# Experts of a two-layer block: two of four token blocks gather their experts' rows, the other two go through all experts

## The chip, the cores and the metric

The kernel runs on one core of a Trainium2 chip. The metric is the time of one execution on the device in microseconds; all data is float32. In the text PE is TensorE (the matrix engine), DVE is VectorE, ACT is ScalarE, POOL is GpSimd, and SP is the queue engine that only issues transfers. Engines run their own instruction lists in order and wait for each other by semaphores.

## The reference, cut to what matters

The whole program is three mixing layers on 512 tokens of width 1024 (convolution, sparse attention, attention and a gated recurrence), then an expert layer, then a small gated layer (called ple). Only the expert layer is changed. There are 16384 experts, each with a row `u` and a row `v` of 1024 numbers. A token picks 16 experts in each of 8 heads, from the sums of two lists of 128 key scores:

```
q = (ht @ w_q).reshape(T, PEER_HEADS, 2, PEER_DKEY // 2)
s = jnp.einsum('thpc,hpnc->thpn', q, sub_keys, preferred_element_type=jnp.float32)
v1, i1 = lax.top_k(s[:, :, 0], K)
v2, i2 = lax.top_k(s[:, :, 1], K)
...
top_s, pos = lax.top_k(cand, K)
idx = jnp.take_along_axis(cand_idx, pos, axis=-1)
g = jax.nn.softmax(top_s, axis=-1)
...
ue = jnp.take(u, ib, axis=0)
a = jnp.einsum('thkd,td->thk', ue, xb, preferred_element_type=jnp.float32)
w = jax.nn.gelu(a) * gb
ve = jnp.take(v, ib, axis=0)
return jnp.einsum('thk,thkd->td', w.astype(ve.dtype), ve)
```

## The kernel before, in words

The 512 tokens are four blocks (b = 0 to 3) of 128 tokens, one token per partition. Everything up to the expert layer is bound to TensorE and stays as it is, apart from its last steps. At the end of the mixing layers PE makes, block by block, the last output product (`merge(b)`: transposes `mT`, then `out_c`), DVE adds it to the residual X (`residual_sum(b)`), normalises the block (`expert_rows(b)`), and PE multiplies by the query weights (`queries`: 32 products of 256 columns for two blocks, then 8 small products with the sub-keys, which give the scores of two heads).

Then comes the expert layer. DVE routes: a group is one head of one block, 32 groups in all, and `route_step(n, k)` does a sixteenth of a group's work (MAX8, FIND_INDEX8, MATCH_REPLACE8 and small operations on HOT). POOL gathers: one indirect transfer brings for the 128 tokens of a block the row `u` of one pick (128 rows of 4 KB, 512 KB), another the row `v`. There are 32 x 16 = 512 picks (PICKS), so 1024 gathers, into rings of 8 buffers each (`U_RING`, `V_RING`). For each pick DVE forms the 128 dot products with the normalised block (L2246), ACT and DVE turn them into weights (`activated`, `weigh`, `weighted`), ACT writes the 16 weights of a group one by one as diagonal matrices (L1446), and PE adds diagonal times gathered rows into PSUM (`expert_row`, L1017, two products of 512 columns per pick). The last of every three picks near the end are added by DVE (L2179). The ple layer follows for each block when its sums are complete (L1079, L1091, `ple_steps`); block 3 comes last, so its ple steps stand at the very end.

The order is written out by hand: DVE's list is one loop over the 512 picks, with the routing of the group two ahead between the dots; POOL's list issues `gather_u(u)` with the `gather_v` that fall due, each after a wait for the buffer.

## Time and profile before

| | us |
|---|---|
| median of 3 runs | 3231.74 (3227.18 to 3245.19) |
| the profiled execution, from its first to its last instruction | 3278.9 |
| PE, DVE, ACT, POOL busy in it | 2812.3, 1829.2, 652.2, 1273.9 |
| granted TensorE clock, mean | 0.967 of full speed |
| moved by transfers | 665.89 MB, 536.94 MB of it by the gathers |

The profiled execution is 47 us longer than the median of the timed runs. Busy time is what an engine spent in instructions; the time of a transfer is not that of the instruction that issues it.

### The profile page before, as it was taken

Reading aid. Unit: us, or ns where it says so; the run is one execution under the profiler, and the core shown is the slowest. Engines: PE = TensorE matmul, PEld = TensorE weight load, DVE = VectorE, ACT = ScalarE, POOL = GpSimd, SP = SyncE. Lnnn points to the kernel's source line nnn. Section 1 sums busy time; section 2 is a strip of 40 time slices with the busy share of each in tenths; the row PEclk is TensorE's granted clock in tenths of the full one; section 3 lists DMA queues with packets and bytes.
Section 4 is the critical chain, followed back from the end, with each engine's and each line's share of the span. In section 5 each row is a group of like instructions: output and inputs, shape, how many; then the busy total and the mean of one; then the engine's idle time right before and its main releaser. Section 6 shows DMA issues by size and latency. Waiting matters only on the chain.

```text
span 3278.9 us, 26326 instructions
## 1 busy us (share of the span) xinstructions
PE 2812.3 (86%) x7932; PEld 1338.4 (41%) x7932; DVE 1829.2 (56%) x4230; ACT 652.2 (20%) x1556; POOL 1273.9 (39%) x1113
## 2 busy tenths in 40 slices
PE   9999999998889899988898889777768786777778
PEld 4455445454554444555555334322223232222323
DVE  4989502058751322267529666576666666666643
ACT  1114301022320112344401111111111111111111
POOL 0520000000000000022104767777777777777774
...
GB/s 179 77 103 52 64 77 77 77 77 26 51 40 77 67 69 51 26 30 49 90 65 216 366 371 368 371 387 373 345 361 371 363 353 367 372 366 352 368 386 244
DMA packets 161469, 665.89 MB, mean 203 GB/s; under 512 B 17856, under 2 KB 18240, under 8 KB 154304
## 3 DMA queue, kind: packets, MB, share of 16 engines
q0 software_dynamic: 147456, 536.94, 43.9%
...
q14 instruction: 64, 0.52, 0.0%
...
## 4 chain that ended last, share of the span: by engine, by line
PE 54%; POOL 18%; issue 9%; DVE 9%; DMA 7%; ACT 2%; another core or an unknown queue 0%; DVEq 0%; ACTq 0%; POOLq 0%; SPq 0%
PE ps L537 13%; PE ps L1017 8%; POOL G L1567 8%; PE ps L652 6%; POOL H L1583 5%; POOL XT L1583 4%; PE ps L589 4%; PE ps L882 3%; DMA XT<-peer_v,C 3%; DMA H<-peer_v,C 3%; PE ps L790 2%; PE ps L911 2%; PE ps L819 2%; DMA G<-peer_u,C 2%; PE ps L976 2%
## 5 line engine op out<-in xcount | busy, mean ns | idle before, releaser
L2246 DVE CUSTOM_DVE_ANT_0 G<-G,H 128x1024 f32<-128x1024 f32 x512 | 627.7, 1226 | 465.7 <-DMA G<-peer_u,C 396.0
L1017 PE MATMUL ps<-H,MK 128*128 128x512 f32 x1196 | 591.2, 623 | 190.3 <-DMA H<-peer_v,C 124.0
L1567 POOL DMA_INDIRECT G<-peer_u,C x512 | 540.3, 1055 | 302.9 <-issue 151.8
L537 PE MATMUL ps<-XT,W 128*128 128x512 f32 (+1 forms) x1344 | 543.0, 553 | 8.9 <-issue 6.5
L1017 PE MATMUL ps<-XT,MK 128*128 128x512 f32 x812 | 403.1, 629 | 130.6 <-DMA XT<-peer_v,C 80.3
L1017 PEld LDWEIGHTS ps<-H,MK 128*128 128x128 f32 x1196 | 218.6, 195 | 532.3 <-issue 476.0
L1583 POOL DMA_INDIRECT H<-peer_v,C x304 | 350.6, 1153 | 131.3 <-issue 71.8
L537 PEld LDWEIGHTS ps<-XT,W 128*128 128x128 f32 x1344 | 254.1, 190 | 294.2 <-issue 286.2
L1017 PEld LDWEIGHTS ps<-XT,MK 128*128 128x128 f32 x812 | 149.5, 197 | 381.1 <-issue 326.0
L1542 POOL COPY PR<-H 128x256 f32<-128x256 f32 x4 | 1.4, 392 | 781.2 <-DVE H L1871 781.2
L1446 ACT ACTIVATE MK<-C 128x128 f32<-128x128 f32 x502 | 175.0, 393 | 524.5 <-PE ps L1017 292.6
L1583 POOL DMA_INDIRECT XT<-peer_v,C x208 | 241.1, 1159 | 78.7 <-issue 48.5
L652 PE MATMUL ps<-W,Y 128*128 128x512 f32 x512 | 226.1, 603 | 13.1 <-DVE Y L1746 6.1
L589 PE MATMUL ps<-XT,W 128*128 128x512 f32 x448 | 220.5, 604 | 1.6 <-ACT G L1152 1.6
L1554 POOL TENSOR_TENSOR H<-H 128x256 f32<-128x256 f32 x56 | 47.6, 852 | 353.9 <-ACT H L1376 320.6
L1645 DVE SCALAR_TENSOR_TENSOR Y<-H,V,Y x240 | 165.3, 765 | 0.0
L652 PEld LDWEIGHTS ps<-W,Y 128*128 128x128 f32 x512 | 98.3, 193 | 140.3 <-issue 137.1
L1433 ACT ACTIVATE H<-C 128x16 f32<-128x16 f32 x32 | 6.9, 216 | 630.3 <-DVE H L2162 336.8
L1528 POOL TENSOR_TENSOR H<-H,SIG 128x512 f32 x12 | 73.5, 6125 | 111.9 <-ACT SIG L1212 108.9
L1755 DVE SCALAR_TENSOR_TENSOR X<-X,H 128x512 f32<-128x512 f32 x16 | 11.1, 691 | 181.9 <-ACT H L1137 181.9
L589 PEld LDWEIGHTS ps<-XT,W 128*128 128x128 f32 x448 | 80.6, 195 | 59.7 <-issue 55.7
L882 PE MATMUL ps<-W,XT 128*128 128x512 f32 x192 | 98.5, 622 | 0.3 <-issue 0.3
...
## 6 DMA issues: line engine op xcount, KB each, us to landing
...
G<-peer_u,C POOLq DMA_INDIRECT x512
...
```

What stands on the lines that cost most here:

```text
L537: mm = pe.matmul(b[:, 0:rhs[k].shape[-1]], w[:, k, m * P:(m + 1) * P], rhs[k], start=(k == 0), stop=(k == KD - 1))
L589: mm = pe.matmul(FILL_BANK[j % 2][:, :], w[:, k, m * P:(m + 1) * P], XT[:, k, :], start=(k == 0), stop=(k == KD - 1))
L652: mm = pe.matmul(ps[pos % 4][:, :], Y[:, (j * KD + k) * T + b * P:(j * KD + k) * T + (b + 1) * P], w[:, k, :], start=(j == 0 and k == 0), ...
L790: mm = pe.matmul(ps[p0 % 4][:, 0:n], XT[:, k, b * P:(b + 1) * P], w[:, k, 0:n], start=(k == 0), stop=(k == KD - 1))
L882: mm = pe.matmul(ring(pos)[:, :], XT[:, k, b * P:(b + 1) * P], w[:, k, :], start=(k == 0), stop=(k == KD - 1))
L1017: mm = pe.matmul(ps[2 * b + half][:, :], DG[by_tensor(v - 1) % DIAG_RING], VB[at][:, half * T:(half + 1) * T], start=(n == FIRST[b] and k ...
L1446: act.activation(DG[at % DIAG_RING], ident, ACT.Copy, scale=GW[:, v:v + 1]).then_inc(diag_full, 1)
L1528: pool.tensor_tensor(hrow(i * 4 + j, TAPS - 1, T), hrow(i * 4 + j, TAPS - 1, T), SIG[:, j, :], ALU.mult).then_inc(glu_done, 1)
L1567: pool.indirect_dma_start(UB[u % U_RING], None, peer_u, bass.IndirectOffsetOnAxis(ap=IDX[:, u:u + 1], axis=0)).then_inc(u_loaded[u % U_RIN ...
L1583: pool.indirect_dma_start(VB[at], None, peer_v, bass.IndirectOffsetOnAxis(ap=IDX[:, v:v + 1], axis=0)).then_inc(v_loaded[at], 16)
L1645: ins = dve.scalar_tensor_tensor(yt(c), hrow(c, k, T), V[:, ds(c * TAPS + (FM["conv_w"] + k), 1)], yt(c), ALU.mult, ALU.add)
L2246: dve.tensor_tensor_reduce(out=rows_u, in0=rows_u, in1=tm(H, 0, D, group(n)[0]), scale=1.0, scalar=0.0, op0=ALU.mult, op1=ALU.add, accum_o ...
```

## The change

Blocks 0 and 1 go on gathering, but another way: their 256 picks (ROWS) are 8 units of 32 (two heads of a block), DVE makes the dot (`row_dot`) and, 8 picks later, also adds the weighted row `v` to X (`row_add`); ACT makes each weight by itself (`row_weight`). No diagonals and no product of PE are left for them. The rings are 3 buffers each for the first 30 picks and 4 after that.

Blocks 2 and 3 take all experts. Twice 128 tiles of 128 experts are read once each by SP into a ring of three buffers of 512 KB (`experts`, a copy of `u` with each tile transposed, then `v`): for each tile of `u` PE multiplies it with both blocks' tokens (`tile_products`, 8 products of 256 columns), ACT applies the gelu (`gelu`) and stores 128 x 256 numbers in GD; for each tile of `v` PE adds the product with GD to four banks (`tile_sums`, 4 products of 512 columns). Between the two, GD must be multiplied by the gates, which are zero but for a token's picks. They are built by PE token by token from two 128 x 128 matrices (`build_pair` makes two tokens; one factor holds the first key's index as ones by DVE, the other the second key's index with the gate by ACT, both called `pair_hot`). These 128 pairs are spread over tiles 73 to 126: tiles not yet made are filled with the gates by ACT (`keep_pair`) and multiplied by the gelu when it comes (`tile_gates`); tiles already there are multiplied on DVE (`pair_gates`). The ple layer is done in the order of blocks 0, 2, 3, 1. The query weights are read twice, once for blocks 0 and 1 and once for 2 and 3. `rows_by(g)` says how many picks DVE has done when it leaves tile g: 34 before the first tile, 77 after tile 68, 91 after the last, so 165 remain for the time after it. Two heads are now routed at once in about 35 steps; 12 of 16 such routings are done by tile 67, four later.

In the diff, blank lines and most helpers are left out.

```diff
+GATHERED = 2
+UNITS = GATHERED * PEER_HEADS // 2
+UNIT_ROWS = 2 * PEER_K
+ROWS = GATHERED * PEER_HEADS * PEER_K
+EARLY_ROWS = 30
+EARLY_RING = 3
+ROW_RING = 4
+LAG = 8
+HELD = 32
+TILES = 128
+STREAM_RING = 3
+PICKED_2, PICKED_3 = 32, 68
...
+def pairs_by(g):
+    if g <= PICKED_3 + 4:
+        return 0
+    return min(128, (g - PICKED_3 - 4) * 128 // (TILES - PICKED_3 - 6))
+def gated(g):
+    return 2 * pairs_by(g - 1)
+def rows_by(g):
+    if g < 0:
+        return 34
+    if g <= PICKED_3:
+        return 34 + (g + 1) * 5 // 8
+    return rows_by(PICKED_3) + (g - PICKED_3) // 4
+def row_before(r):
+    if r < EARLY_ROWS:
+        return r - EARLY_RING if r >= EARLY_RING else None
+    return r - ROW_RING if r >= EARLY_ROWS + ROW_RING else EARLY_ROWS - 1
+def route_quota(g):
+    first, second = min(1.0, (g + 1) / (PICKED_2 - 1)), max(0.0, min(1.0, (g + 1 - PICKED_2) / (PICKED_3 - PICKED_2 - 1)))
+    return int(ROUTE_STEPS * (2 + 5 * first + 5 * second))
...
+            sp.wait_ge(bank_full, POS["xT_f2"] + 2)
+            for m in range(2 * TILES):
+                if m == 2:
+                    sp.wait_ge(x_spilled, 16)
+                if m >= STREAM_RING:
+                    last = m - STREAM_RING
+                    if last < TILES:
+                        sp.wait_ge(a_full, last + 1)
+                    else:
+                        sp.wait_ge(v_used, last + 1 - TILES)
+                sp.dma_start(STREAM[m % STREAM_RING][:, :], experts[m]).then_inc(streamed[m % STREAM_RING], 16)
...
             queries("wq0a", 0, (0, 1))
             merge(2)
+            queries("wq1a", 1, (0, 1))
             merge(3)
-            queries("wq1a", 1, (0, 1))
+            queries("wq2a", 2, (0, 1))
+            queries("wq3a", 3, (0, 1))
...
+            def tile_products(g):
+                u = STREAM[g % STREAM_RING][:, :].rearrange("p (k e) -> p k e", k=KD)
+                pe.wait_ge(streamed[g % STREAM_RING], 16 * (g // STREAM_RING + 1))
+                if g >= 2:
+                    pe.wait_ge(gelu_done, g - 1)
+                for k in range(KD):
+                    mm = pe.matmul(UP_BANK[g % 2][:, 0:256], u[:, k, :], XTD[:, k, :], start=(k == 0), stop=(k == KD - 1))
+                mm.then_inc(a_full, 1)
+            def build_pair(p):
+                pe.wait_ge(pair_one1, p + 1)
+                pe.wait_ge(pair_one2, p + 1)
+                if p >= 2:
+                    pe.wait_ge(pair_gated, p - 1)
+                for i in range(2):
+                    mm = pe.matmul(BUILD_BANK[p % 2][:, i * P:(i + 1) * P], ONE_2[:, (2 * p + i) % 4, :],
+                                   ONE_1[:, (2 * p + i) % 4, :], start=True, stop=True)
+                mm.then_inc(built, 1)
+            def tile_sums(i):
+                m = TILES + i
+                pe.wait_ge(streamed[m % STREAM_RING], 16 * (m // STREAM_RING + 1))
+                for b in range(2):
+                    for n in range(2):
+                        mm = pe.matmul(acc(b, n)[:, :], GD[:, i * 256 + b * P:i * 256 + (b + 1) * P],
+                                       STREAM[m % STREAM_RING][:, n * T:(n + 1) * T], start=(i == 0), stop=(i == TILES - 1),
+                                       skip_group_check=True)
+                        if i == TILES - 1:
+                            mm.then_inc(acc_full, 1)
+                if i < TILES - 1:
+                    mm.then_inc(v_used, 1)
...
+            tile_products(0)
+            for g in range(TILES):
+                if g + 1 < TILES:
+                    tile_products(g + 1)
+                for b in (2, 3):
+                    if g == (PICKED_2, PICKED_3)[b - 2] + 1:
+                        picks_transposed(b)
+                for p in pairs_of(g):
+                    build_pair(p)
+            pe.wait_ge(pair_gated, TILES)
+            pe.wait_ge(tile_gated, sum(gated(g) > 0 for g in range(TILES)))
+            pe.wait_ge(it_copied, 2)
+            for i in range(TILES):
+                tile_sums(i)
+                if i == 96:
+                    ple_transposes(0)
+                if i in (100, 101):
+                    ple_gates(0, i - 100)
+                if i == 103:
+                    ple_proj(0)
+            for i in range(1, 4):
+                ple_transposes(i)
+                ple_gates(i, 0)
+                ple_gates(i, 1)
+                ple_proj(i)
...
+            def row_weight(r):
+                at = r % HELD
+                if r % UNIT_ROWS == 0:
+                    act.wait_ge(unit_gates, r // UNIT_ROWS + 1)
+                act.wait_ge(dots, r + 1)
+                act.activation(ACTED[:, at:at + 1], DOT[:, at:at + 1], ACT.Gelu_apprx_tanh).then_inc(acted, 1)
+                act.wait_ge(acted, r + 1)
+                act.activation(WEIGHT[:, at:at + 1], ACTED[:, at:at + 1], ACT.Copy, scale=GW[:, r:r + 1]
+                               ).then_inc(weights, 1)
...
+            def gelu(g):
+                n = gated(g)
+                act.wait_ge(a_full, g + 1)
+                if g == 64:
+                    act.wait_ge(unit_in, 4)
+                    act.wait_ge(scores_out, 16)
+                if g == 80:
+                    act.wait_ge(soft_in, 1)
+                if g == 88:
+                    act.wait_ge(soft_in, 2)
+                if g == 32:
+                    act.wait_ge(v_added, EARLY_ROWS)
+                if n > 0 and gated(g - 2) > 0:
+                    act.wait_ge(tile_gated, sum(gated(a) > 0 for a in range(g - 1)))
+                if n > 0:
+                    ins = act.activation(WA[g % 2][:, 0:n], UP_BANK[g % 2][:, 0:n], ACT.Gelu_apprx_tanh)
+                if n < 256:
+                    ins = act.activation(GD[:, g * 256 + n:(g + 1) * 256], UP_BANK[g % 2][:, n:256], ACT.Gelu_apprx_tanh)
+                ins.then_inc(gelu_done, 1)
+            def pair_hot(p):
+                if p >= 2:
+                    act.wait_ge(built, p - 1)
+                if p == 0:
+                    act.wait_ge(it_copied, 2)
+                for i in range(2):
+                    t = 2 * p + i
+                    act.activation(ONE_2[:, t % 4, :], IOTA, ACT.Abs, scale=-1.0, bias=IT[:, 1, t:t + 1]).then_inc(act_link, 1)
+                    ac.n += 1
+                for i in range(2):
+                    t = 2 * p + i
+                    ac.after(ac.n - 1 + i)
+                    ins = act.activation(ONE_2[:, t % 4, :], ONE_2[:, t % 4, :], ACT.Relu, scale=IT[:, 3, t:t + 1],
+                                         bias=IT[:, 2, t:t + 1])
+                ins.then_inc(pair_one2, 1)
+            def keep_pair(p, g):
+                act.wait_ge(built, p + 1)
+                act.activation(DENSE[:, 2 * p:2 * p + 2, g + 1:TILES],
+                               BUILD_BANK[p % 2][:, 0:256].rearrange("p (t i) -> p t i", t=2)[:, :, g + 1:TILES], ACT.Copy
+                               ).then_inc(gates_kept, 1)
...
+            for g in range(TILES):
+                gelu(g)
+                for b in (2, 3):
+                    at_step = (PICKED_2, PICKED_3)[b - 2]
+                    if g == at_step:
+                        exponentials(b)
+                    if g == at_step + 2:
+                        picks_copied(b)
+                for p in pairs_of(g):
+                    keep_pair(p, g)
+                for p in pairs_of(g + 1):
+                    pair_hot(p)
+                row_weights(rows_by(g) - LAG)
...
+                if r == rows_by(TILES - 1) + 30:
+                    act.wait_ge(v_used, 68)
...
-            for u in range(PICKS):
-                for v in range(v_issued(u), v_issued(u + 1)):
-                    gather_v(v)
-                gather_u(u)
-            for v in range(v_issued(PICKS), PICKS):
-                gather_v(v)
+            for r in range(ROWS + LAG):
+                if r < ROWS:
+                    gather_u(r)
+                if r >= LAG:
+                    gather_v(r - LAG)
...
+            def row_dot(r):
+                at, uses = row_place(r)
+                dve.wait_ge(u_loaded[at], 16 * uses)
+                if r >= HELD:
+                    dve.wait_ge(weights, r - HELD + 1)
+                dve.tensor_tensor_reduce(out=ROW_U[at][:, :], in0=ROW_U[at][:, :], in1=XN[:, r // P, :], scale=1.0,
+                                         scalar=0.0, op0=ALU.mult, op1=ALU.add,
+                                         accum_out=DOT[:, r % HELD:r % HELD + 1]).then_inc(dots, 1)
+            def row_add(r):
+                at, uses = row_place(r)
+                b = r // P
+                dve.wait_ge(v_loaded[at], 16 * uses)
+                dve.wait_ge(weights, r + 1)
+                if r > 0:
+                    dve.wait_ge(v_added, r)
+                dve.scalar_tensor_tensor(X[:, b, :], ROW_V[at][:, :], WEIGHT[:, r % HELD:r % HELD + 1], X[:, b, :],
+                                         ALU.mult, ALU.add).then_inc(v_added, 1)
+                if r % P == P - 1:
+                    dve.wait_ge(v_added, r + 1)
+                    dve.sem_inc(x_out[b], 2)
+            def rows_to(end):
+                nonlocal softened, done_rows
+                while done_rows < end:
+                    r = done_rows
+                    while routed < UNITS and 32 * routed - r <= 10:
+                        draw_to(drawn + 1)
+                    if softened < UNITS and r - LAG == 32 * softened - 8:
+                        unit_softmax(softened)
+                        softened += 1
+                    row_dot(r)
+                    if r >= LAG:
+                        row_add(r - LAG)
+                    done_rows += 1
...
+            def pair_gates(p, g):
+                dve.wait_ge(gates_kept, p + 1)
+                view = DENSE[:, 2 * p:2 * p + 2, 0:g + 1]
+                dve.tensor_tensor(view, view, BUILD_BANK[p % 2][:, 0:256].rearrange("p (t i) -> p t i", t=2)[:, :, 0:g + 1],
+                                  ALU.mult).then_inc(pair_gated, 1)
...
+            residual_sum(2)
+            unit_softmax(0)
+            row_factor(2)
+            residual_sum(3)
+            row_factor(3)
+            for r in range(rows_by(-1)):
+                if r >= 6:
+                    draw_to(min(36 * 2, 36 + 3 * (r - 5)))
+                rows_to(r + 1)
...
+            for g in range(TILES):
+                draw_to(route_quota(g))
+                for b in (2, 3):
+                    at_step = (PICKED_2, PICKED_3)[b - 2]
+                    if g == at_step - 1:
+                        while blocks_routed < b:
+                            draw_to(drawn + 1)
+                    if g == at_step:
+                        soft_end(b)
+                if gated(g) > 0:
+                    tile_gates(g)
+                for p in pairs_of(g):
+                    pair_gates(p, g)
+                for p in pairs_of(g + 1):
+                    pair_hot(p)
+                rows_to(rows_by(g))
+            for r in range(rows_by(TILES - 1), ROWS):
+                at_row = r - rows_by(TILES - 1)
```

How the lists of the engines stand now. The first place is on DVE after the routing of the first heads. Before (L2075 is `residual_sum(2)`, L2246 the dot):

```order
L2153 CAST C<-H 128x16
L2075 TENSOR_TENSOR X<-X,ps 128x512 x2
L1819 ISA H,ST<-X 128x1024
L1819 ISA ST 128x1
L2078 TENSOR_SCALAR ST<-ST 128x1
L2246 ISA G,H<-G,H 128x1024
L2246 ISA H 128x1
```

Now (L2299 are `residual_sum(2)` and `residual_sum(3)`, L2305 `row_factor`, which waits for ACT's root, L2454 the dot):

```order
L2395 TENSOR_TENSOR UNIT_EX<-UNIT_BG 128x32
L2299 TENSOR_TENSOR X<-X,ps 128x512 x2
L2402 TENSOR_REDUCE SMX<-UNIT_EX 128x2
L2403 RECIPROCAL SMX<-SMX 128x2
L2404 TENSOR_TENSOR C<-UNIT_EX,SMX 128x32
L2305 RECIPROCAL ST<-ST 128x1
L2299 TENSOR_TENSOR X<-X,ps 128x512 x2
L2305 RECIPROCAL ST<-ST 128x1
L2454 ISA EARLY_U_69,DOT<-EARLY_U_69,XN 128x1024
L2454 ISA DOT 128x1
```

The first dot stood behind the residual of block 2 alone; it now stands behind the residuals and factors of both blocks 2 and 3.

The second place is PE. Before, after the sub-keys of the third `queries`, L537 is a product of the query weights and L1017 an expert row's two products:

```order
L1034 MATMUL ps<-MK,SIG 128x128 x8
L537 MATMUL ps<-XT,W 128x256
L1017 MATMUL ps<-H,MK 128x512 x2
L537 MATMUL ps<-XT,W 128x256
L1017 MATMUL ps<-H,MK 128x512 x2
```

Now, at the last tiles of `u` and the first of `v` (L1135 `tile_products`, L1154 `build_pair`, L1164 `tile_sums`):

```order
L1135 MATMUL ps<-XTD,STREAM_62 128x256 x8
L1154 MATMUL ps<-ONE_63,ONE_64 128x128 x6
L1135 MATMUL ps<-XTD,STREAM_60 128x256 x8
L1154 MATMUL ps<-ONE_63,ONE_64 128x128 x4
L1135 MATMUL ps<-XTD,STREAM_61 128x256 x8
L1154 MATMUL ps<-ONE_63,ONE_64 128x128 x6
L1164 MATMUL ps<-STREAM_62,GD 128x512 x4
L1164 MATMUL ps<-STREAM_60,GD 128x512 x4
```

A tile of `u` is followed by two or three pairs, each two products of 128 columns; a pair is built only behind the products of the tile after its own.

The third place is ACT at tile 112 of `u`. Before, its list in the expert layer was this (L1446 are the diagonals, L1433 and L1434 the group's exponentials and tanh):

```order
L1434 ACTIVATE H<-H 128x16
L1446 ACTIVATE MK<-C 128x128 x16
L1433 ACTIVATE H<-C 128x16
L1434 ACTIVATE H<-H 128x16
L1446 ACTIVATE MK<-C 128x128 x16
```

Now (L1628 and L1630 `gelu`, L1653 `keep_pair`, L1641 and L1646 the two halves of `pair_hot`, L1584 and L1586 `row_weight`):

```order
L1628 ACTIVATE C<-ps 128x184
L1630 ACTIVATE GD<-ps 128x72
L1653 ACTIVATE GD<-ps 128x2x15 x2
L1641 ACTIVATE ONE_64<-C,IT 128x128 x2
L1646 ACTIVATE ONE_64<-ONE_64,IT 128x128 x2
L1641 ACTIVATE ONE_64<-C,IT 128x128 x2
L1646 ACTIVATE ONE_64<-ONE_64,IT 128x128 x2
L1641 ACTIVATE ONE_64<-C,IT 128x128 x2
L1646 ACTIVATE ONE_64<-ONE_64,IT 128x128 x2
L1584 ACTIVATE ACTED<-DOT 128x1
L1586 ACTIVATE WEIGHT<-ACTED,C 128x1
L1628 ACTIVATE V<-ps 128x188
```

One tile's share is two gelus, two kept pairs and here three `pair_hot` for the next tile, the third of which has to wait until PE has built the first of these three.

## Rows read from the trace of the kernel before

**Rows 1.** Stretch 1900:3200, busy PE, PEld, DVE, ACT, POOL; clock, DMA share, GB/s.

```profile
1900.00:3200.00 1300.00, 985.46 (x2105) 385.03 (x2106) 837.48 (x2143) 194.11 (x574) 981.73 (x891) 0.96 0.98 367
```

**Rows 2.** The page's transfers: GB/s in 40 slices of 82 us, and the gathers' queue.

```profile
GB/s 179 77 103 52 64 77 77 77 77 26 51 40 77 67 69 51 26 30 49 90 65 216 366 371 368 371 387 373 345 361 371 363 353 367 372 366 352 368 386 244
...
q0 software_dynamic: 147456, 536.94, 43.9%
```

**Rows 3.** Groups by line and shape, 1700 to 3279 us: what a pick costs each engine.

```profile
L2246 DVE CUSTOM_DVE_ANT_0 G<-G,H 128x1024 f32<-128x1024 f32 x512 | 627.7, 1226 | 465.7 <-DMA G<-peer_u,C 396.0 <-issue 40.7 <-remote 11.4
...
L1567 POOL DMA_INDIRECT G<-peer_u,C x512 | 540.3, 1055 | 302.9 <-issue 151.8 <-DVE C L2153 129.0 <-DVE H L2246 21.8
...
L2179 DVE SCALAR_TENSOR_TENSOR X<-XT,C,X 128x1024 f32<-128x1024 f32 x5 | 6.4, 1285 | 16.6 <-DMA XT<-peer_v,C 13.5 <-issue 3.1
```

**Rows 4.** PE in order of time: start, length, instruction.

```profile
1704.95 14.05 PE L537 MATMUL ps<-XT,W 128*128 128x256 f32 x64 [0.89 <-issue]
1719.47 2.05 PE L1034 MATMUL ps<-MK,SIG 128*128 128x128 f32 x16 [0.47 <-ACT SIG L1490]
1721.36 1.04 PE L575 MATMUL ps<-C,MK 128*128 128x128 f32 x8
...
1730.38 7.03 PE L988 MATMUL ps<-H,XT 128*128 128x512 f32 x16
...
1807.16 1.88 PE L1017 MATMUL ps<-H,MK 128*128 128x512 f32 x4
```

**Rows 5.** DVE in order of time: the routing of a head, and the first dots.

```profile
1722.24 0.62 DVE L2116 MAX8 H<-Y 128x8 f32<-128x128 f32 x2 [18.86 <-ACTq L1494]
...
1733.17 0.62 DVE L2116 MAX8 H<-Y 128x8 f32<-128x128 f32 x2
...
1746.98 1.23 DVE L2246 CUSTOM_DVE_ANT_0 G<-G,H 128x1024 f32<-128x1024 f32 x1
...
1780.24 1.23 DVE L2246 CUSTOM_DVE_ANT_0 G<-G,H 128x1024 f32<-128x1024 f32 x1
1781.39 0.08 DVE L2246 DVE_READ_ACCUMULATOR2_ANT H<- 128x1 f32 x1
```

**Rows 6.** Groups by line and shape, 1700 to 3279 us: routing on DVE.

```profile
L2116 DVE MAX8 H<-Y 128x8 f32<-128x128 f32 x128 | 37.4, 292 | 24.1 <-ACTq L1494 18.9 <-DVE H L2116 3.1
L2118 DVE FIND_INDEX8 H<-H,Y 128x8 uint32<-128x128 f32 x128 | 36.4, 285 | 0.0
...
L2116 DVE MAX8 H<-H 128x8 f32<-128x256 f32 x64 | 27.1, 423 | 0.1
L2144 DVE TENSOR_TENSOR H<-H,C 128x256 f32<-128x256 f32 x64 | 26.9, 421 | 0.1
...
L2118 DVE FIND_INDEX8 H<-H 128x8 uint32<-128x256 f32 x64 | 26.8, 418 | 0.0
L2120 DVE MATCH_REPLACE8 Y<-H,Y 128x128 f32<-128x128 f32 x64 | 17.6, 275 | 0.0
```

**Rows 7.** ACT in order of time: diagonals, copies from PSUM; a table load.

```profile
2309.91 1.28 ACT L1446 ACTIVATE MK<-C 128x128 f32<-128x128 f32 x4 [3.64 <-DVE C L2171]
...
3258.98 1.14 ACT L1455 ACTIVATE Y<-ps,V 128x128 f32<-128x128 f32 x4 [16.16 <-PE ps L1079]
3260.13 1.28 ACT L1450 ACT_TABLE_LOAD   x1
```

**Rows 8.** All engines in order of time: the end.

```profile
3252.47 1.28 DVE L2179 SCALAR_TENSOR_TENSOR X<-XT,C,X 128x1024 f32<-128x1024 f32 x1 [3.89 <-DMA XT<-peer_v,C]
...
3257.54 1.29 DVE L2187 TENSOR_TENSOR X<-X,ps 128x512 f32<-128x512 f32 x2 [3.79 <-PE ps L1017]
...
3260.26 13.97 PE L1091 MATMUL ps<-W,Y 128*128 128x512 f32 x32 [0.72 <-ACT Y L1455]
```

**Rows 9.** PE in order of time, where the granted clock fell.

```profile
1587.24 2.04 PE L911 MATMUL ps<-H 128*128 128x128 f32 x8 [3.51 <-POOL H L1554]
...
1594.41 1.05 PE L911 MATMUL ps<-H 128*128 128x128 f32 x8
```

880 lines of the change are left out of this document (478 added, 402 removed), and 4 rows, old and new, of the table at.

## The prediction

> **What bounds the kernel now.** I read the stretches first: from 1900 to 3200 us the transfers are busy 98% of the time at 367 GB/s, while PE is busy 76%, POOL 76%, DVE 64% and ACT 15% [rows 1]. The 40 slices say the same: from slice 22 on they show 345 to 387 GB/s [rows 2]. The gathers took 43.9% of 3278.9 us on all 16 engines for 536.94 MB, so 373 GB/s if nothing but they run. Then the cost of a pick: the dots waited 396 us for their rows [rows 3]. The expert layer is bound by transfers: 1024 gathers of 0.524 MB at 1.43 us each.
>
> **What goes away.** 512 of 1024 gathers, 268 MB, against 2 x 128 tiles of 0.524 MB, 67 MB for u and 67 MB for v: 134 MB less, and a second reading of the query weights, 8 MB more. At 367 GB/s that is 343 us less, if the transfers stayed busy. They do not, so I sum the new layer stage by stage, in the profile's own time.
>
> **Prices.** PE: 64 of the profile's instructions, 32 products of 256 columns in the program, took 14.05 us, and four, which are two of 512, 1.88 us with 1.72 from start to start [rows 4]. So a product of 256 columns is 0.43 us and one of 512 is 0.86: a tile of u costs 8 x 0.43 = 3.45 us, a tile of v 4 x 0.86 = 3.43. Sixteen instructions on the sub-keys took 2.05 us, so a pair (four) is 0.51. DVE: a dot is 1.15 us to the next instruction, 1.23 by itself [rows 5]; an add 1.29, of which I count 1.2 [rows 3]. Routing one head took 10.9 us, 1722.24 to 1733.17 [rows 5]. Two heads at once, from the same kinds of instruction [rows 6] with 0.04 between: eight MAX8, eight FIND_INDEX8 (with its 0.09 of loading) and four MATCH_REPLACE8 on 128 numbers 7.4, the sums 0.6, the same on 256 numbers 5.0, three operations on 1024 cells 3.5 (a multiply of 256 is 0.42, most of it per number), small ones 1.4: 17.5 us for two heads. ACT: four diagonals took 1.28 us, four copies of 128 from PSUM 1.14 [rows 7]: a `pair_hot` is 1.3, a kept pair 0.25, the two gelus of a tile 0.55.
>
> **Start of the picks.** The first keys are scored at 1721.5, and `merge(2)` ends at 1737.4 [rows 4]. DVE's list now puts two factors ahead of the first dot. The factor of block 3 needs: `queries` (14.05 + 0.5 + 2.05 = 16.6) to 1754, ACT's root and scaling of block 2, which stand ahead of its copies of block 3 (4 us, an estimate from ACT's rows, one table load of 1.28 among them [rows 7]), `merge(3)` 16, the third `queries` 16.6, the root 2: 1792. The first dot was at 1747 [rows 5]. DVE waits in between with three rows already there: 45 us lost at the outset.
>
> **34 picks before the first tile.** DVE 34 x 1.15 + 26 x 1.2 + 17.5 = 88 us. Transfers: 57 gathers, four slots of 2.1 MB of weights, 2 MB of spills and three tiles: 42 MB, 115 us. With rings of three I take 118, to 1910 (bounds 90 and 140).
>
> **Tiles 0 to 67.** DVE has 10 routings, 174 us, and 42 picks of 2.35, 99, and a few waits: 275 us, 4.05 a tile. PE needs 3.45 a tile, transfers (0.52 + 0.66 MB) 3.2. DVE bounds it: 2185. The way over to the pairs is 18 us: block 3's softmax, transposes and copies, then tiles 71 to 74 at PE's pace because ACT may only run two banks behind, and two pairs: 2203.
>
> **Tiles 74 to 126 with pairs.** Here the transfers have 0.8 MB a tile to do, 2.2 us, and stand idle. In 33 tiles with two pairs PE is the longest: 3.45 + 1.02 = 4.5. In 20 tiles there are three. ACT's third `pair_hot` waits until PE has built the first of the three, behind the next tile's products, at 4.2 after the last pair; then 1.3 for ACT, 0.55 gelu, 0.25 keep, 0.5 DVE's `pair_gates`, which must come before the third pair's bank is reused, and 0.6 for PE: 7.5. With picks on DVE in a quarter of them 33 x 4.5 + 20 x 7.5 + 7 = 305 us, and 3 to the last product: 2511. Nothing in the trace shows such a chain; the bounds are PE alone (53 x 4.7 = 249) and every tile at 7.5 (398). I stay between, as the list of ACT gives it.
>
> **The rest of the picks beside v.** 165 picks remain: 330 gathers, 125 tiles, 7.5 MB of ple weights and parked data: 246 MB, 669 us at 367. PE's 128 tiles need 439 us, 153 GB/s, so they are hidden. Added: ACT may not weigh pick 121 before tile 68 of v is used, at 233 us; the picks get 367 - 153 = 214 GB/s, 4.9 us each, and arrive there after 185. About 50 us in which only v moves cost 28. The last steps (routing beside the picks: 3.0 a pick against 2.85, last eight adds) 9. In sum 706: 3217.
>
> By the Trainium skill ("DMA: Bandwidth & Descriptors", section on the anatomy of one DMA) a transfer costs about 2.0 us and its bytes at 436 GB/s; this trace's highest slice has 387 [rows 2]. By that figure these 246 MB would take 564 us and the kernel end near 3155; I go by the slices.
>
> **The end.** Before, the last row is added at 3252.5, block 3's sums at 3257.5, and 32 instructions of gates ran 3260.3 to 3274.2 [rows 8]; the end is 3278.9. Now two blocks stand behind the last add, since DVE's `ple_scale` for the third comes after it: 1.3 + 13.9 gates + 3.5 projection + 1.4 transposes + 1.2 + 13.9 + 3.5, and 4.5 for the store: 43. Sum: 3260 against 3278.9, 0.6% less; by the ratio 0.9942 to the median 3231.74: 3213 us.
>
> **Rivals.** (a) The pairs hand over worse: each hop between ACT, PE and DVE costs as much in the tiles with two. Then all 53 tiles take 7.5 us: 398 for 305, 3353, in the median 3305. It turns slower by 0.5% from 6.4 us a tile. For it: four engines are in the chain, with two buffers each. Against it: with two pairs all of ACT's 3.1 us fits under PE's 3.45. Chance 0.22. (b) The transfers lose by mixing two queues: at the lowest full slice's 345 GB/s [rows 2] 713 for 669: 3304, median 3256. Against: 367 held with both kinds of gathers. Chance 0.08. (c) It goes better: pairs at PE's pace (56 less) or the pick start earlier and the stall at pick 121 less: 3205, median 3159. For it: ACT and DVE are used by less than four fifths there, and every stall I added comes from reading lists, not from a row. Chance 0.26. (d) PE falls to 1.2 GHz because it now waits for others between tiles: after a gap of 3.5 us eight instructions took 2.04 us for 1.05 [rows 9]. In the tiles PE waits 0.6 of 4.05 us, so I expect none; if it stayed low, 68 tiles of 6.9 for 4.05 are 194 us and the pairs' tiles 180 more: 3630. Chance 0.03.
>
> The Trainium skill ("TensorE: Matmul & The Clock Gate", Part 1) says that the clock depends on how busy the engine has lately been; at 76% busy the trace has 0.96 [rows 1], which agrees with no fall here.
>
> (e) That the change saves nothing at all, because GD's reads and writes go across the rows in steps of 1 KB and cost DVE and ACT double: `pair_gates` and `keep_pair` 0.4 more a pair, in the chain of the 20 tiles 16 us: 3276, no change. Chance 0.03.
>
> **How the numbers follow.** The sum as it stands, within 25 us, has 0.38; 3262 is the border of 0.5% (16 us, about what a measurement of this kernel can tell from no change), so 0.20 of it is faster, 0.17 within and 0.01 slower. Faster: 0.20 + 0.26 = 0.46. Within: 0.17 + (e) 0.03 + 0.02 of (a) = 0.22. Slower: 0.20 of (a), 0.08 of (b), 0.03 of (d) and 0.01 of the forecast = 0.32. The range leaves out the upper half of (a) with (d), and the tail of (c): 3130 to 3300. The forecast's own is 3188 to 3238.
>
> **What would show each step.** The first dot near 1792, and DVE waiting for ACT's root before it; the last `tile_products` near 2510; between tiles 0 and 67 DVE over 90% busy; from 2200 to 2510 transfers under 200 GB/s; a gap of PE of about 3 us in every tile with three pairs; v's tiles at 3.4 us and the picks beside them at 4.9; a wait of ACT at pick 121 of some 50 us; two rows of gates of 14 us behind the last add. I am wrong if the pairs run at another pace than 5.75 us a tile, if the start of the dots is another, or if the last 700 us do not run at 367 GB/s.

## The result, and the profile after

| | us |
|---|---|
| before, median of 4 runs | 3229.66 (3227.18 to 3245.19) |
| after, median of 4 runs | 3268.64 (3261.09 to 3282.64) |
| ratio | 1.0118, interval 1.0088 to 1.0148 |
| the profiled execution after, first to last instruction | 3259.0 |

Beside these runs the changed kernel is 1.2% slower; the forecast was 0.6% faster. Its profiled execution is the fastest of its four; that of before (3278.9) was 49 us above the median of its runs. The forecast's sum in the profile's time was 3260.

The stretches of after, with busy PE, PEld, DVE, ACT and POOL, then clock, DMA share and GB/s, as in [rows 1]:

```profile
1740.00:1910.00 170.00, 155.74 (x722) 127.94 (x721) 81.30 (x148) 49.35 (x138) 64.68 (x58) 0.96 0.72 269
1910.00:2185.00 275.00, 234.39 (x1054) 199.37 (x1053) 253.68 (x723) 50.24 (x159) 124.58 (x97) 0.93 0.87 315
2185.00:2510.00 325.00, 272.09 (x1357) 239.85 (x1356) 154.05 (x336) 218.82 (x755) 24.19 (x26) 0.91 0.42 132
2510.00:2950.00 440.00, 414.12 (x968) 179.45 (x968) 259.60 (x454) 68.16 (x233) 193.37 (x173) 0.98 0.90 350
2950.00:3220.00 270.00, 94.29 (x211) 40.74 (x211) 230.25 (x340) 57.28 (x185) 183.88 (x160) 0.67 0.94 356
```

Where before one resource bounds the whole layer, four now take turns: waits at the start, DVE (254 of 275 us) beside the tiles of u, PE with a lower clock beside the pairs, where transfers are busy 0.42, and the transfers and DVE in the last two. The page's transfers, to be read against [rows 2]:

```profile
GB/s 181 78 103 52 65 77 78 77 56 48 26 65 74 59 77 55 26 27 37 70 95 74 355 351 315 292 304 129 128 131 123 374 409 174 411 409 409 361 349 158
DMA packets 125770, 544.51 MB, mean 167 GB/s; under 512 B 13888, under 2 KB 14272, under 8 KB 117568
...
q0 software_dynamic: 73728, 268.47, 21.9%
q1 hardware_dynamic: 49472, 258.02, 21.5%
```

Counted from 1, slices 28 to 31 (123 to 131) are the pairs, and slice 34 (174) is a stall. DVE at the start, in order of time, against [rows 5]; in brackets the idle time before and what ended it:

```profile
1757.85 0.16 DVE L2305 RECIPROCAL ST<-ST 128x1 f32<-128x1 f32 x1 [18.35 <-ACT ST L1545]
1770.24 0.69 DVE L2299 TENSOR_TENSOR X<-X,ps 128x512 f32<-128x512 f32 x1 [12.23 <-PE ps L1060]
1777.11 0.69 DVE L2299 TENSOR_TENSOR X<-X,ps 128x512 f32<-128x512 f32 x1 [6.18 <-PE ps L1060]
1795.68 0.16 DVE L2305 RECIPROCAL ST<-ST 128x1 f32<-128x1 f32 x1 [17.88 <-ACT ST L1545]
1795.76 1.21 DVE L2454 CUSTOM_DVE_ANT_0 EARLY_U<-EARLY_U,XN 128x1024 f32<-128x1024 f32 x1
```

The waits of after between 2205 and 2500 us (engine, line, whom it waited for: us in sum, times, longest):

```profile
ACT GD L1653 <- PE ps L1154: 77.6, 70, 3.1
...
PE ps L1154 <- DVE GD L2517: 50.3, 18, 3.9
DVE ONE L2508 <- PE ps L1154: 36.5, 17, 2.4
ACT ONE L1641 <- PE ps L1154: 16.6, 17, 1.0
```

PE's product of a tile of u, the pairs' broadcast and the sums over v in after, with durations (min, median, max) and first and last start:

```profile
L1135 PE MATMUL ps<-XTD,STREAM x2048: 379/379/636, 1884.0 to 2516.0; 128*128 128x256 f32 x187
...
L1154 PE MATMUL ps<-ONE,ONE x512: 272/275/554, 2193.9 to 2520.2; 128*128 128x128 f32 x171
...
L1164 PE MATMUL ps<-STREAM,GD x1024: 592/592/1191, 2521.9 to 3017.9; 128*128 128x512 f32 x171
```

ACT and DVE at pick 121, where ACT waits for tile 68 of v (L2466 is the add), and then PE behind the last add, against [rows 8]:

```profile
2768.29 0.20 ACT L1584 ACTIVATE ACTED<-DOT 128x1 f32<-128x1 f32 x1 [124.35 <-issue]
```

```profile
2768.91 1.28 DVE L2466 SCALAR_TENSOR_TENSOR X<-ROW_V,WEIGHT,X 128x1024 f32<-128x1024 f32 x1 [88.79 <-issue]
```

```profile
3216.01 15.98 PE L1191 MATMUL ps<-GD 128*128 128x512 f32 x32 [23.84 <-issue]
3231.84 3.60 PE L1201 MATMUL ps<-GD 128*128 128x512 f32 x8
3235.27 1.04 PE L1180 MATMUL ps<-C,X 128*128 128x128 f32 x8
3237.57 13.97 PE L1191 MATMUL ps<-GD 128*128 128x512 f32 x32 [1.26 <-ACT GD L1667]
```

After ScalarE's wait of 124.4 us is over, it works off ten weights in 4 us. DVE had gone on for the first 36 us of that wait, with the weights it already had, and then stood still for 88.8 us.

### The profile page after: what moved, and what is told of

Same layout as the page of the kernel before. It is cut to its first block, busy times and chain, and to the rows that moved or that the text cites. A ratio compares the mean times of both kernels' runs of the same rounds, so it can differ in the third digit from the quotient of the medians.

```text
span 3259.0 us, 29551 instructions
## 1 busy us (share of the span) xinstructions
PE 2834.4 (87%) x9642; PEld 1656.4 (51%) x9642; DVE 1828.8 (56%) x3752; ACT 877.9 (27%) x2363; POOL 735.3 (23%) x601
## 3 DMA queue, kind: packets, MB, share of 16 engines
q0 software_dynamic: 73728, 268.47, 21.9%
## 4 chain that ended last, share of the span: by engine, by line
PE 61%; DMA 12%; DVE 10%; issue 8%; POOL 5%; ACT 3%; DVEq 0%; ACTq 0%; SPq 0%; POOLq 0%
PE ps L609 15%; PE ps L1135 11%; PE ps L724 6%; DMA ROW_U<-peer_u,C 5%; DMA ROW_V<-peer_v,C 4%; PE ps L661 4%; PE ps L954 3%; DMA STREAM<-experts 2%; POOL ROW_U L1799 2%; POOL ROW_V L1808 2%; PE ps L862 2%; PE ps L983 2%; PE ps L891 2%; PE ps L1060 2%; PE ps L1154 2%
## 5 line engine op out<-in xcount | busy, mean ns | idle before, releaser
L1135 PE MATMUL ps<-XTD,STREAM 128*128 128x256 f32 x2048 | 481.9, 395 | 5.3 <-DMA STREAM<-experts 4.9
L1164 PE MATMUL ps<-STREAM,GD 128*128 128x512 f32 x1024 | 452.8, 600 | 16.6 <-DMA STREAM<-experts 14.9
L1135 PEld LDWEIGHTS ps<-XTD,STREAM 128*128 128x128 f32 x2048 | 401.4, 199 | 70.5 <-DMA STREAM<-experts 14.2
L1799 POOL DMA_INDIRECT ROW_U<-peer_u,C x226 | 273.8, 1211 | 530.7 <-DVE DOT L2454 499.0
L2466 DVE SCALAR_TENSOR_TENSOR X<-ROW_V,WEIGHT,X 128x1024 f32<-128x1024 f32 x226 | 290.1, 1284 | 182.3 <-issue 105.8
L1164 PEld LDWEIGHTS ps<-STREAM,GD 128*128 128x128 f32 x1024 | 190.5, 191 | 277.1 <-issue 207.6
L1808 POOL DMA_INDIRECT ROW_V<-peer_v,C x226 | 250.9, 1110 | 245.1 <-DVE X L2466 201.6
L2454 DVE CUSTOM_DVE_ANT_0 ROW_U<-ROW_U,XN 128x1024 f32<-128x1024 f32 x226 | 275.5, 1219 | 43.4 <-DMA ROW_U<-peer_u,C 41.6
L1584 ACT ACTIVATE ACTED<-DOT 128x1 f32<-128x1 f32 x256 | 51.0, 199 | 551.6 <-DVE DOT L2454 426.5
L1154 PE MATMUL ps<-ONE,ONE 128*128 128x128 f32 x512 | 74.9, 288 | 55.4 <-DVE GD L2517 55.4
L1646 ACT ACTIVATE ONE<-ONE,IT 128x128 f32<-128x128 f32 x256 | 110.9, 482 | 0.0
```

Source lines behind the costliest of these rows:

```text
L1135: mm = pe.matmul(UP_BANK[g % 2][:, 0:256], u[:, k, :], XTD[:, k, :], start=(k == 0), stop=(k == KD - 1))
L1154: mm = pe.matmul(BUILD_BANK[p % 2][:, i * P:(i + 1) * P], ONE_2[:, (2 * p + i) % 4, :], ONE_1[:, (2 * p + i) % 4, :], start=True, stop=True)
L1164: mm = pe.matmul(acc(b, n)[:, :], GD[:, i * 256 + b * P:i * 256 + (b + 1) * P], STREAM[m % STREAM_RING][:, n * T:(n + 1) * T], start=(i == ...
L1646: ins = act.activation(ONE_2[:, t % 4, :], ONE_2[:, t % 4, :], ACT.Relu, scale=IT[:, 3, t:t + 1], bias=IT[:, 2, t:t + 1])
L1799: pool.indirect_dma_start(ROW_U[at][:, :], None, peer_u, bass.IndirectOffsetOnAxis(ap=IDX[:, r:r + 1], axis=0)).then_inc(u_loaded[at], 16)
L1808: pool.indirect_dma_start(ROW_V[at][:, :], None, peer_v, bass.IndirectOffsetOnAxis(ap=IDX[:, r:r + 1], axis=0)).then_inc(v_loaded[at], 16)
```

## The experiments

**The kernel before, profiled again.** Three runs of unchanged kernels ask what the first profile was worth. `e1_before` and `e11_before` are the kernel before, `e10_after` the changed one.

> The kernel before, unchanged, profiled a second time. Theory A: the profile that the sum was scaled by (3278.9 us) caught an execution whose gathers ran slower than in the timed runs; a second profile has a span near 3228 us and the gathers of 1900 to 3200 us at some 380 GB/s instead of 367. Rival B: the profiler always lengthens this kernel, by what it records of the gathers; the span is 3279 us again and only the timed runs are near 3230.

> The kernel before, unchanged and profiled a third time. It ran at 3226 to 3230 us in three sets of runs and at 3278 us in a fourth, and the changed kernel at 3269 and 3265 us. Theory (all runs of the kernel before within one set of runs lie at one of two levels, some 50 us apart, which its gathers make: its first profile, 3278.9 us, was of the upper one): this kernel agrees with the other runs of before in its set within 0.3 percent, whichever level they have; at the lower one its gathers run at 367 to 383 GB/s after 1900, at the upper one at 360 to 375. Rival (the upper level was one disturbed set, and single executions vary as much): times spread from 3205 to 3290 within the set.

> The changed kernel, unchanged and profiled a second time. Theory (stretches in which only gathers run differ from one execution to the next, as 361 to 368 against 367 to 379 GB/s in the two profiles of the kernel before; stretches with the stream beside the gathers do not): time 3260 to 3275, the span within 25 us of 3259, 405 to 412 GB/s again between 2800 and 3000, and what differs lies between 3000 and 3200. Rival (the second half of the changed kernel is bound by something other than its gathers): both profiles alike within 5 us everywhere.

| | median us | runs beside it | profiled span |
|---|---|---|---|
| e1_before | 3222.88 | before 3229.30 (3204.19 to 3241.49, 25 runs) | 3239.5 |
| e11_before | 3224.44 | before 3228.25 (3219.37 to 3242.49, 13 runs) | 3222.7 |
| e10_after | 3265.35 | before 3278.46 (3268.21 to 3292.82, 13 runs) | 3256.8 |

The kernel before has two levels: in four sets of runs its median is 3226 to 3230 and no run is above 3246, in two others (this one and that of `e12_sums` below) it is 3278 and 3283 and no run is below 3268. The changed kernel was at 3269 and 3265, on either side. So the ratio is 1.0118 against the lower level and 0.9966 (0.9944 to 0.9988) against the upper. The first profile of before (3278.9) has the length of the upper level; no execution was profiled beside timed runs of that level, so that it belongs there is argued from its length and its rates. The rival of `e1_before`, that the profiler lengthens this kernel, is excluded: the two new profiled executions took 3239.5 and 3222.7 us. The rival of `e11_before`, that single executions vary from 3205 to 3290 us within one set, is excluded too. The same stretch as [rows 1] in `e1_before` and in `e11_before`:

```profile
1900.00:3200.00 1300.00, 1010.24 (x2170) 392.70 (x2171) 849.68 (x2158) 201.76 (x598) 997.76 (x919) 0.96 0.99 378
```

```profile
1900.00:3200.00 1300.00, 1024.53 (x2204) 402.55 (x2204) 853.52 (x2162) 202.36 (x599) 987.36 (x922) 0.96 0.99 379
```

They read 378 and 379 GB/s where the first profile has 367. 12 GB/s over 1300 us are 15.6 MB, 41 us at 379; `e11_before` is 56 us shorter than the first. The changed kernel, profiled twice, has the same rates in both (first `after`, then `e10_after`):

```profile
2800.00:2900.00 100.00, 91.98 (x215) 38.52 (x213) 74.57 (x126) 16.76 (x58) 56.29 (x50) 0.98 1.03 409
...
3000.00:3100.00 100.00, 17.56 (x40) 6.97 (x38) 92.41 (x154) 19.56 (x71) 72.53 (x64) 0.61 0.97 366
```

```profile
2800.00:2900.00 100.00, 89.87 (x211) 37.85 (x211) 75.65 (x130) 18.56 (x60) 51.42 (x50) 0.97 1.03 409
...
3000.00:3100.00 100.00, 17.59 (x40) 7.13 (x40) 91.62 (x148) 19.21 (x69) 71.34 (x64) 0.61 0.97 366
```

Beside the stream it is 409 GB/s; where gathers run alone, 366 with DVE busy 92 of 100 us. The two levels stand in the timed runs of the kernel before. The changed kernel is alike beside both (spans 3259.0 and 3256.8), and so are its stretches, which was the rival of `e10_after`, and not its theory. That this is because its gathers seldom bound it is argued from the rows; what makes the level is open. Two of the sets, one at each level, ran on a chip of the same number, so a difference between chips is not shown to be it.

**ScalarE's wait later.** ACT's wait for tile 68 of v stands 36 picks later in `e2_later`, with block 0's ple steps 30 picks later.

```diff
-                if r == rows_by(TILES - 1) + 30:
+                if r == rows_by(TILES - 1) + 66:
                     act.wait_ge(v_used, 68)
...
```

> ACT's wait for tile 68 of v moves from pick 121 to pick 157, and the ple steps of block 0 on ACT and DVE 30 picks later. Theory A (the wait of 124 us holds DVE's adds and with them the gathers, and the transfers do only v meanwhile): 3268 us falls by 30 to 55, to about 3225. Rival B (the transfers or PE's tiles of v bound the stage anyway and the picks catch up): within 8 us of 3268.

3205.93 us, ratio to before 0.9935 (0.9912 to 0.9958), 63 less than after. The last add started at 3157.1 against 3213.4 (56 us), and the wait of 124.4 us is gone. The stretch in which after had stood still, first of `after`, then of `e2_later`:

```profile
2700.00:2750.00 50.00, 50.00 (x118) 22.23 (x117) 0.00 (x0) 0.00 (x0) 0.00 (x0) 1.00 0.48 150
2750.00:2800.00 50.00, 41.25 (x95) 17.25 (x93) 17.23 (x29) 6.46 (x30) 12.30 (x12) 1.00 0.83 323
```

```profile
2700.00:2750.00 50.00, 48.68 (x112) 20.50 (x112) 35.84 (x61) 6.46 (x26) 26.27 (x25) 1.00 1.03 409
2750.00:2800.00 50.00, 46.60 (x106) 19.08 (x104) 34.90 (x57) 8.27 (x25) 30.06 (x23) 1.00 1.03 414
```

DVE's zero becomes 36 of 50 us. The stall was worth more than the 30 to 55 us expected: the v tiles last until 3053.8 instead of 3017.9, so the 409 GB/s of the mixed stretch also reach further into the picks. How much of the gain each of the two is, no run separates.

**Two pairs in every tile.** The pairs begin ten tiles earlier in `e3_even`.

```diff
-PICKED_2, PICKED_3 = 32, 68
+PICKED_2, PICKED_3 = 32, 58
...
-        return 34 + (g + 1) * 5 // 8
+        return 34 + (g + 1) * 3 // 4
```

> Block 3 is routed by tile 57 instead of 67 and the picks beside the first tiles go a little faster, so that the 128 pairs stand two to each of 64 tiles and no tile has three. Theory A (a tile with three pairs takes 7.5 us because the third goes round ACT, PE, DVE and PE again, one with two takes 4.5): the stages of u end 20 to 35 us earlier, 3240 us. Rival B (every pair costs the same 2.4 us wherever it stands): no gain within 8 us.

3206.06 us, 0.9946 (0.9920 to 0.9972), 62 less than after, twice the expectation. The last product with u starts at 2462.9 against 2516.0, 53 us earlier; the edit also does four picks more (95 for 91, by `rows_by`) before the tiles of v, which is argued to be the rest.

**Four banks for the broadcast.** `e8_banks` keeps the pairs where they were but lets PE run four pairs ahead of DVE's product with the gates.

```diff
-        UP_BANK, BUILD_BANK, IT_BANK = (ps[0], ps[1]), (ps[2], ps[3]), ps[4]
+        UP_BANK, BUILD_BANK, IT_BANK = (ps[0], ps[1]), (ps[2], ps[3], ps[5], ps[6]), ps[4]
...
-                if p >= 2:
-                    pe.wait_ge(pair_gated, p - 1)
+                if p >= 4:
+                    pe.wait_ge(pair_gated, p - 3)
...
```

> The changed kernel with four PSUM banks for the gates' broadcast, so that TensorE waits for VectorE's gates of the pair four before instead of two before. In the changed kernel TensorE waited 50.3 us in 18 waits for VectorE's gates between 2205 and 2500. Theory (that wait makes a tile of three pairs 7 us long): 30 to 50 us less. Rival (the chain through ScalarE and VectorE's one-hot rows, of which two buffers stay, holds TensorE as long): 8 us less at most.

3209.02 us, 0.9942 (0.9916 to 0.9968), 60 less than after, where 30 to 50 were expected; its last product with u starts at 2461.0 against 2516.0. Two things changed. PE of after in order of time, around a tile with three pairs:

```profile
2385.09 1.20 PE L1154 MATMUL ps<-ONE,ONE 128*128 128x128 f32 x4 [3.73 <-DVE GD L2517]
2386.08 5.87 PE L1135 MATMUL ps<-XTD,STREAM 128*128 128x256 f32 x16
2391.79 1.05 PE L1154 MATMUL ps<-ONE,ONE 128*128 128x128 f32 x8
2392.68 3.62 PE L1135 MATMUL ps<-XTD,STREAM 128*128 128x256 f32 x16
```

After a wait of 3.73 us for DVE, the next tile's sixteen instructions take 5.87 us, and 3.62 in the tile after that. Not every wait has this behind it: after 10 of the 16 waits between 2205 and 2460 us the next sixteen took 4.7 to 6.1 us, after the other six (waits of 2.3 to 3.5 us) 3.62. The groups of PE from 2205 to 2460 us, first of `after`, then of `e8_banks`:

```profile
L1135 PE MATMUL ps<-XTD,STREAM 128*128 128x256 f32 x668 | 168.8, 411 | 0.0
L1154 PE MATMUL ps<-ONE,ONE 128*128 128x128 f32 x392 | 58.0, 290 | 43.9 <-DVE GD L2517 43.9
```

```profile
L1135 PE MATMUL ps<-XTD,STREAM 128*128 128x256 f32 x811 | 183.9, 380 | 0.7
L1154 PE MATMUL ps<-ONE,ONE 128*128 128x128 f32 x476 | 65.7, 278 | 21.9 <-issue 21.9
```

PE's wait for DVE, 43.9 us in 16 waits of up to 3.8 us, is gone; 21.9 us of shorter ones, up to 1.2 us each, remain. The profile names nobody for these; by the lists PE waits there for ACT's third one-hot pair, which would be the rival's chain, real but not the whole. The other half is the clock: it was 0.91 of full speed over 2185 to 2510 in after, and 1.00 without the long waits. 9% of 255 us are 23 us, and the waits are 22 us shorter; scaled to the 322 us of the pairs, 57, against 55 measured. Part of the tile that followed a wait ran at the lower level of 1.2 GHz. The Trainium skill ("TensorE: Matmul & The Clock Gate", Part 1) says that the clock depends on how busy the engine has been, and the trace agrees.

**DVE takes eight dots earlier.** In `e4_early` four dots stand before the residual of block 3 and four more before its factor:

```diff
+            rows_to(4)
             residual_sum(3)
+            rows_to(8)
             row_factor(3)
...
```

> The changed kernel, with VectorE doing the dots of picks 0 to 7 before the third residual sum and row factor of the first stage instead of after them. In the changed kernel two reciprocals of VectorE are idle 18.35 and 17.88 us ahead of the first dots. Theory (the first dot starts at 1795.8 only because VectorE does the third row block first, and everything up to the last pick hangs on it): first dot some 10 us earlier and the time 8 to 10 us less than the changed kernel. Rival (the first stage of picks is bound by what they bring in, not by when the first starts): no difference, 3 us at most.

3249.34 us, 1.0077 (1.0054 to 1.0099). By medians this is 19 less than after, by the profiled spans (3248.9 and 3259.0) 10. The first pair starts 16 us earlier, 2177.6 against 2193.9, the last add 10 us, 3203.3 against 3213.4. The rival, 3 us at most, is excluded, and the size is the theory's (8 to 10) by the spans, more by the medians. But the first dot starts at 1758.1 against 1795.8, 38 us earlier and not 10, and most of that is gone before the pairs: what follows doesn't hang on the first dot alone.

**Block 3's gates before the last five adds.** The index of `ple_scale` and `ple_factor` is the place in the order of blocks 0, 2, 3, 1, so 2 means block 3. In `e5_tail`:

```diff
                 row_add(r)
+                if r == ROWS - 6:
+                    ple_scale(2)
+                    ple_factor(2)
-            for i in (2, 3):
-                ple_scale(i)
-                ple_factor(i)
+            ple_scale(3)
+            ple_factor(3)
```

> DVE's scaling of the third block's transposed rows stands six adds ahead of the end instead of behind the last. Theory A (two blocks' gates, 14 us each with 3.5 of projection, stand behind the last add): 12 to 17 us less, 3253 us. Rival B (PE is not ready for the third block's gates earlier, or the last adds are late for it): under 4 us.

3258.48 us, 1.0109 (1.0065 to 1.0153), 10 less than after by the medians (7 less than `e10_after`); the profiled spans are only 1.9 apart (3257.1 and 3259.0). The span hides the gain, because this execution was already 6 us later before anything that the edit changes. The same step of block 2's output on DVE (L2555), first in `after`, then in `e5_tail`:

```profile
3189.46 0.69 DVE L2555 TENSOR_TENSOR GD<-GD 128x512 f32<-128x512 f32 x1
```

```profile
3195.52 0.69 DVE L2555 TENSOR_TENSOR GD<-GD 128x512 f32<-128x512 f32 x1
```

From there to the end it is 61.6 us against 69.5, 8 less. The first row of gates starts 2.7 us earlier than in after, so 8.7 earlier counted from that step, and is 0.84 us longer:

```profile
3213.33 16.82 PE L1191 MATMUL ps<-GD 128*128 128x512 f32 x32 [15.10 <-issue]
```

The gain is under the theory's 12 to 17 us and over the rival's 4; the gates start only 8 us before the end of the last add, since DVE's step stands in its list behind the add of 3210.9.

**The edits together.** `e6_all` has e2, e3, e4 and e5.

> Four edits together: the later wait of ScalarE (alone -63 us against the changed kernel), two pairs in every tile (alone -62), the early dots, and the second block's tail six sums before the end (alone -10). Theory (the first two gains lie in different stages, after 2500 and before it, and add): 3269 - 63 - 62 - 10 - 8 = 3126, with 3120 to 3150 as the range. Rival (both gains are the same time, since either one only moves the moment from which gathers alone bound the rest): 3190 to 3205, no better than either alone.

3113.08 us, ratio 0.9656 (0.9603 to 0.9709). By the medians the four add: 3268.6 - 63 - 62 - 19 - 10 is 3115. The result lies below the theory's range (3120 to 3150), which counted 8 us for the early dots. By the profiled spans the four alone give 56 + 58 + 10 + 2 = 126 us, together 150.5 (3108.5). Either way the rival, that the first two are the same time, is excluded.

`e7_more` also puts a pick beside every second instead of every fourth tile of pairs.

```diff
-    return rows_by(PICKED_3) + (g - PICKED_3) // 4
+    return rows_by(PICKED_3) + (g - PICKED_3) // 2
```

> All four edits, and beside the pair tiles one row of picks every two steps instead of every four, so 17 more picks lie in the stage where the transfers were busy 0.40. Theory (that stage has free transfer time and free VectorE time): each pick moved there is taken off the last stage at its 2.3 to 2.8 us there, so 30 to 48 us less than the four edits together. Rival (TensorE was busy 100 percent of that stage with two pairs a tile, and VectorE hands over the gates of every pair: each row ahead of a hand-over holds TensorE for its 2 to 3 us): the gain is 0 to 10 us.

3098.13 us, 0.9604 (0.9551 to 0.9658): 15 less than `e6_all`, where 30 to 48 were expected. The last u product came 7 us later (2452.5 against 2445.4), and the last add only 9.9 us earlier (3062.7 against 3072.6). The gain lies between the theory's and the rival's (0 to 10). From 2950 on the transfers are no longer full in it:

```profile
2900.00:2950.00 50.00, 48.96 (x114) 20.70 (x112) 36.38 (x49) 6.96 (x28) 37.19 (x30) 1.00 1.03 410
2950.00:3000.00 50.00, 43.42 (x105) 18.78 (x104) 14.94 (x20) 2.24 (x10) 9.50 (x9) 0.99 0.67 247
```

DVE is busy 15 of 50 us there, because `add_sums` stands at a fixed place, 20 picks before the last, and with more picks done early it comes before PE's last sums over v:

```profile
2990.64 1.48 DVE L2534 TENSOR_TENSOR GD<-GD,ps 128x512 f32<-128x512 f32 x2 [31.74 <-PE ps L1164]
```

`e12_sums` moves it eight picks back, and block 2's gated steps behind it. It also takes back the edit of `e5_tail`, so block 3's gates stand behind the last add again.

```diff
-                if r == ROWS - 20:
+                if r == ROWS - 12:
                     add_sums(2)
                     add_sums(3)
...
```

> The kernel with the denser rows (3098 us), in which VectorE takes the sums over v of blocks 2 and 3 eight picks later, 12 before the last instead of 20, with the gated layer's steps of block 2 behind them. There VectorE waited 31.7 us for TensorE's last sums over v, with 20 picks left, while the transfers fell to 247 GB/s. Theory (this wait is why the denser rows brought 15 us and not 30 to 48): eight picks of 2.35 us, 19 us, now lie before the wait, of which the later gates of block 2 cost at most half: 8 to 19 us less than 3098. Rival (the two blocks' gates, 14 us each, that can only begin after the sums over v set the end): 0 to 5 us less, or up to 10 more.

3091.32 us beside a before at 3282.93 (ratio 0.9415, interval 0.9396 to 0.9434), 7 less than `e7_more`, one below the theory's range (8 to 19) and above the rival's (0 to 5). The transfers stay full until 3000:

```profile
2950.00:3000.00 50.00, 43.82 (x105) 18.46 (x104) 34.41 (x44) 6.46 (x26) 24.03 (x25) 1.00 1.03 409
```

So the 31.7 us were a loss, but only 7 us came of it: the three rows of gates behind the sums, 15.77, 16.94 and 13.97 us with their waits, now fill the time from 3010 to the end. What the edit of `e5_tail` would be worth here was not tried.

`e9_both` adds the four banks to `e7_more`.

> The four edits and the denser rows (3098 us), and the four banks for the gates' broadcast (alone 60 us less than the changed kernel, twice what was expected). Theory (the four banks and the even tiles remove the same wait, that of TensorE for VectorE's gates, and with two pairs in every tile none of it is left in the trace between 2205 and 2500, where only the rows beside the pairs can still bring some): 0 to 8 us less than 3098. Rival (the banks' gain came from somewhere else and adds): 30 to 60 us less.

3100.13 us, 2 more than `e7_more`: nothing is left of the banks' 60 us. Even tiles and more banks remove the same wait.

## Why the prediction was wrong

**The step that failed** is the last one: "Sum: 3260 against 3278.9, 0.6% less; by the ratio 0.9942 to the median 3231.74: 3213 us". The sum itself came out, 3260 for a span of 3259.0. But it was divided by the time of a profile that lies above every timed run shown beside it (3245.19). 3278.9 fits the upper level of the kernel before; the changed kernel does not follow that level, having run at 3269 us beside the lower and 3265 beside the upper. Beside runs of the upper level the ratio was 0.9966 (0.9944 to 0.9988), near the forecast's 0.9942. Against the timed median, 3260 is 0.9% slower; measured, 1.2%. The text named the 47 us, and took them as a scale of everything. Where the kernel before spends most of them is shown by `e11_before` (379 for 367 GB/s from 1900 to 3200, 41 us); why one execution has the one rate and another the other stays open.

That the sum came out within 1 us of the profiled execution was partly luck: every stage ends within 10 us of its forecast, but within the last one two errors cancelled.

| step | forecast | after |
|---|---|---|
| first dot | 1792 | 1795.8 |
| tile 67, pairs begin | 2185, 2203 | first pair 2193.9 |
| last product with u | 2511 | 2516.0 |
| rate of the transfers beside v | 367 GB/s | 409 with the stream, 366 alone |
| DVE's adds stand still at pick 121 | 50 us | 88.8 us (ACT's own wait 124.4) |
| a tile of v | 3.43 us | 3.88 us (496 us for 128) |
| end of the last add | 3217 | 3214.7 |
| from there to the end | 43 | 44.3 |

**The start** is as forecast, within 4 us: two waits of 18 us for ACT's root and two for `merge(3)` [rows 4, 5]. The parts of a routing of two heads add up to 17.9 us in the prediction and not 17.5, 4 us over ten of them.

**The pairs.** 305 us were forecast for 53 tiles, of them 20 with three pairs at 7.5 us. The chain exists as described, with PE waiting for `pair_gates`, and its length was nearly right: from one tile's products to the next it is 7.3 to 7.9 us in a tile with three pairs, and 8.5 to 9.3 in the six where a pick on DVE stands just ahead. What the forecast lacked is the lower clock in the tile behind many of these waits. From the first pair to the last it is 326 us with the chain, 275 without (`e3_even`, over 64 tiles) and 270 with four banks. Rival (a) was not it, since tiles with two pairs ran at PE's pace, 4.35 us in the trace; rival (d) came in part, as a mean of 0.91 of full speed rather than half, which is 23 of 255 us, about as much as the waits that four banks took away. Of rival (e), DVE's product with the gates took 587 ns mean for the 0.5 us counted.

**The stall.** The forecast's 185 us fit 38 picks of 4.9 us (the 30 to pick 121 and the lag of 8), so its 50 us are to be compared with DVE's 88.8 and not with ACT's 124.4. Both ends of it were off. The picks came there 164 us after the last product with u (2680.0), 21 sooner: DVE began them only at 2533, but the rows of the first four stood in the rings already, and from 2550 on the transfers ran faster than 367 GB/s:

```profile
2550.00:2680.00 130.00, 127.35 (x291) 53.31 (x290) 95.18 (x159) 14.73 (x51) 72.81 (x66) 1.00 1.03 409
```

Tile 68 of v was used at 2765, and the adds went on at 2768.9, 253 us after the last product with u and not 233. Behind the stall the stream and the gathers moved 410 GB/s until 3018; against 367 that is an estimated 29 us gained (43 GB/s over 250 us, divided by 367), and it gave back about what the longer stall took, which is argued and was not run. By the Trainium skill ("DMA: Bandwidth & Descriptors", "Where 436 GB/s comes from") the memory side gives a core about 358 GB/s and binds such transfers, and the ports into SBUF allow 435. The trace doesn't agree with the first: 409 to 414 GB/s over 50 to 130 us exceed it, and the measurement decides; they keep below the second. Rival (b), a loss by mixing, is excluded: mixing gained.

**Where the 121.4 MB went** (665.9 to 544.5). At the 379 GB/s of `e11_before` they are 320 us. The stretches of `e11_before`:

```profile
1740.00:1910.00 170.00, 143.25 (x454) 80.67 (x454) 128.02 (x322) 24.99 (x73) 112.12 (x103) 0.96 0.91 339
1910.00:2185.00 275.00, 235.06 (x556) 98.71 (x555) 179.91 (x470) 43.34 (x134) 205.71 (x192) 0.97 1.00 385
2185.00:2510.00 325.00, 250.39 (x528) 96.05 (x526) 226.03 (x591) 52.33 (x155) 251.66 (x235) 0.96 1.00 382
2510.00:2950.00 440.00, 327.61 (x680) 124.55 (x680) 299.47 (x778) 66.73 (x201) 339.35 (x315) 0.96 0.99 375
2950.00:3220.00 270.00, 218.75 (x462) 86.41 (x460) 146.58 (x320) 45.24 (x119) 183.65 (x176) 0.94 0.91 349
```

Against after's five rows above, rate difference times length: 11.9, 19.3, 81.3, 11.0 and -1.9 MB less moved, together 121.6. In time at 379 GB/s: 31 us behind the late first dot, 51 beside DVE's routing, 214 beside the pairs, 29 with the stall, -5. So the whole saving was used up by transfers standing idle, two thirds of it in the stage of the pairs, and the end (36 us after 3222.7, two blocks' gates) made it slower.
